# FFN up: three pairs of slabs in seven products before each ordinary pair, where seven-product and ordinary pairs alternated

## The reference

```python
h = x @ w_up                                   # 512 x 1024 by 1024 x 5632
h = conv(h, conv_w, width 3, causal, per channel) + conv_b
gate, val = split(h, 2)
out = (silu(gate) * val) @ w_down              # 2816 x 1024
```

## Time and profile before

| what | us |
|---|---|
| median of three executions | 2039.16 |
| the profiled execution | 2042.29 |
| its span | 2040.6 |
| TensorE busy | 2026.4 |
| VectorE busy | 1619.3 |
| ScalarE busy | 1115.0 |
| GpSimd busy | 433.7 |

### The profile page before, as it was taken

How to read it: one execution, slowest core, us unless ns; L and a number is a source line. 1 busy time by engine, 2 the same in 40 slices (tenths; PEclk the granted TensorE clock), 3 DMA queues, 4 the chain that set the end, 5 groups by cost and what they waited for, 6 DMA issues and landing times.

```text
span 2040.6 us, 33333 instructions
## 1 busy us (share of the span) xinstructions
PE 2026.4 (99%) x12636; PEld 1750.7 (86%) x12636; DVE 1619.3 (79%) x2555; ACT 1115.0 (55%) x1861; POOL 433.7 (21%) x482
## 2 busy tenths in 40 slices
PE   9999999999999999999999999999999999999998
PEld 8889998888988899888877888998888889999887
DVE  6668878889467887899888669777997668877898
ACT  4755545447335555546656646555465755545555
POOL 0520332210000232120035402322110520332220
PEclk9999999999999999999999999999999999999999
DMA  8123344384432334467421123334674122334393
GB/s 291 64 104 125 109 130 150 121 255 172 145 129 75 97 105 129 145 190 243 166 73 42 63 83 104 119 104 155 197 237 163 65 104 83 109 122 147 115 269 122
DMA packets 82570, 276.42 MB, mean 135 GB/s; under 512 B 9408, under 2 KB 13632, under 8 KB 82032
## 3 DMA queue, kind: packets, MB, share of 16 engines
q1 hardware_dynamic: 59184, 214.67, 30.4%
q0 software_dynamic: 11200, 24.12, 5.8%
q10 hardware_dynamic: 12032, 35.54, 4.8%
HBM read 256.43 MB, written 14.73 MB: 133 GB/s over the span
## 4 chain that ended last, share of the span: by engine, by line
PE 91%; DVE 5%; DMA 2%; ACT 1%; issue 0%; DVEq 0%; ACTq 0%; SPq 0%
PE ps L2437 12%; PE ps L2438 12%; PE ps L2439 12%; PE ps L2649 6%; PE ps L3018 5%; PE ps L3019 5%; PE ps L3020 5%; PE ps L2976 5%; PE ps L2978 5%; PE ps L2977 5%; PE ps L2509 2%; PE ps L2465 2%; PE ps L2466 2%; PE ps L2467 2%; DMA raw<-slabs 2%; PE ps L2497 1%
## 5 line engine op out<-in xcount | busy, mean ns | idle before, releaser
L2437 PE MATMUL ps<-h_hi,w_hi 128*128 128x512 f32 (+1 forms) x1104 | 433.0, 392 | 0.0
L2438 PE MATMUL ps<-h_lo,w_hi 128*128 128x512 f32 (+1 forms) x1104 | 429.6, 389 | 0.0
L2439 PE MATMUL ps<-h_hi,w_lo 128*128 128x512 f32 (+1 forms) x1104 | 428.9, 389 | 0.0
L1603 DVE TENSOR_TENSOR w_lo<-raw,w_hi 128x1024 fp32r<-128x1024 f32 x300 | 372.0, 1247 | 39.1 <-ACT w_hi L901 35.5
L901 ACT ACTIVATE w_hi<-raw 128x1024 fp32r<-128x1024 f32 x312 | 326.4, 1053 | 133.1 <-DVE raw L2251 74.0
L2437 PEld LDWEIGHTS ps<-h_hi,w_hi 128*128 128x128 f32 x1104 | 207.6, 188 | 44.0 <-issue 4.0
L2439 PEld LDWEIGHTS ps<-h_hi,w_lo 128*128 128x128 f32 x1104 | 207.3, 188 | 43.2
L2438 PEld LDWEIGHTS ps<-h_lo,w_hi 128*128 128x128 f32 x1104 | 207.7, 188 | 38.9
L1281 ACT ACTIVATE work<-ps,conv_sb 128x512 f32<-128x512 f32 x120 | 93.0, 775 | 162.6 <-PE ps L2439 133.2
L3018 PE MATMUL ps<-w_hi,h_hi 128*128 128x512 f32 x408 | 159.7, 391 | 2.1 <-DVE w_lo L1603 2.1
L3020 PE MATMUL ps<-w_hi,h_lo 128*128 128x512 f32 x408 | 158.8, 389 | 0.0
(11 more groups left out here) (365 smaller groups left out, 5054.6 us busy)
## 6 DMA issues: line engine op xcount, KB each, us to landing
raw<-slabs SPq DMA_DIRECT2D x368, 512.0 KB, 4.1
act<-slabs POOLq DMA_DIRECT2D x64, 256.0 KB, 5.6
bias<-slabs SPq DMA_DIRECT2D x16, 512.0 KB, 6.3
x_dram<-x ACTq DMA_DIRECT2D x16, 512.0 KB, 5.0
x<-x_dram ACTq DMA_DIRECT2D x16, 512.0 KB, 4.9
raw<-act POOLq DMA_DIRECT2D x28, 256.0 KB, 3.3
act<-slabs SPq DMA_DIRECT2D x12, 512.0 KB, 5.4
bias_dram<-bias_rows ACTq DMA_DIRECT2D x2, 2048.0 KB, 12.3
```

The source lines that it names most:

```text
L1603: ve.tensor_tensor(w_lo[:, c % RING, :], raw[:, raw_slot(c), :], w_hi[:, c % RING, :].bitcast(f32), ALU.subtract).then_inc(lo_made, 1)
L2437: pe.matmul(ps[:, bank, cols], hi, h_hi[:, k, cols], start=k == 0, stop=False)
L2438: pe.matmul(ps[:, bank, cols], hi, h_lo[:, k, cols], start=False, stop=False)
L2439: last = pe.matmul(ps[:, bank, cols], lo, h_hi[:, k, cols], start=False, stop=k == KT - 1)
```

## The change

Pairs 7, 11 and 15 of each layer become seven-product pairs too: 4, then the groups 6-7-8-(9), 10-11-12-(13), 14-15-16-(17), in which the pair in brackets is ordinary. TensorE's products of neighbouring seven-product pairs are interleaved (lists at the end of the diff), and four pairs of PSUM banks are used in turn. The orders of ScalarE and VectorE are written anew as `first_period` (pairs 4 and 5 and the start of the first group), `period` (twice) and `last_period` (the last group and the end of the stage to pair 21). SP's loads follow the new order. GpSimd starts the sums for FFN down only when the adding transfer issued before them has landed (`landed`). One wait for `up_mm` is added to `split_hi`, one for `up_x3` to `x2`, and the negated convolution weights are made in four instructions instead of one. Shown are the core of the diff and the starts of the long lists; `part_hi`, `part_lo`, `copy`, `c11`, `c22` and `c12` do what they did, with their counts adapted.

```diff
 FAST, FAST_END = 4, 18
-FASTS = (FAST_END - FAST) // 2
+FAST_RUNS = 6, 10, 14
+IN_GROUP = 3
+FAST_PAIRS = [FAST] + [q + e for q in FAST_RUNS for e in range(IN_GROUP)]
+FASTS = len(FAST_PAIRS)
+X1_ORDER = [FAST] + [q + e for q in FAST_RUNS for e in (1, 0, 2)]
+UP_PRODUCTS = [(FAST, p) for p in (1, 2, 6, 4, 3)] + [
+    (q + e, p) for q in FAST_RUNS for e, p in (
+        (0, 1), (0, 2), (0, 6), (1, 1), (1, 2), (0, 4), (0, 3), (1, 6), (2, 1), (1, 4), (2, 2), (1, 3), (2, 6),
+        (2, 4), (2, 3))]
 PARTS = "a11", "x1", "x2", "x3", "x4"
 STEPS = FFT // 2
...
 
-            return (0 if q // 2 % 2 else 4) + e
+            return 2 * ((q + 2) % 4 if FAST <= q < FAST_END else q % 2) + e
...
+                def load(q, e):
+
+                    c = up_slab(L, q, e)
+                    if q - 2 not in FAST_PAIRS:
+                        sp.wait_ge(lo_made, made(c - RAW))
+                    elif e:
+                        sp.wait_ge(part_lo_made["x3"], part_count(L, q - 2, "x3"))
+                        sp.wait_ge(part_lo_made["x4"], part_count(L, q - 2, "x4"))
+                    else:
+                        sp.wait_ge(part_lo_made["x1"], part_count(L, q - 2, "x1"))
+                        sp.wait_ge(up_x2, fast(L, q - 2) + 1)
+                        sp.wait_ge(up_x3, fast(L, q - 2) + 1)
+                    sp.dma_start(raw[:, raw_slot(c), :], slabs[dram(c)]).then_inc(raw_in[raw_slot(c)], 16)
+
...
-            def down_sums(L, j):
+            def down_sums(L, j, landed=None):
...
                     pool.wait_ge(in_lo, 4 * (L + 1))
+                if landed:
+                    pool.wait_ge(up_x4, 16 * (fast(L, landed) + 1))
...
+                fourth_sum(L, 4)
+                down_sums(L, 0, 4)
+                fourth_sum(L, 6)
+                down_sums(L, 1, 6)
+                fourth_sum(L, 7)
+                fourth_sum(L, 8)
+                down_sums(L, 2, 8)
+                fourth_sum(L, 10)
+                down_sums(L, 3, 10)
+                fourth_sum(L, 11)
+                fourth_sum(L, 12)
+                down_sums(L, 4, 12)
+                fourth_sum(L, 14)
+                down_sums(L, 5, 14)
+                fourth_sum(L, 15)
+                fourth_sum(L, 16)
+                down_sums(L, 6, 16)
+                for j in range(7, STEPS - 1):
                     down_sums(L, j)
...
                     sc.wait_ge(w_used, 4 * i + (c - (RING + EARLY if early(c - RING) else RING) + 1))
+                if isinstance(i, int) and in_fast(c - RING):
+                    L, q, e = in_fast(c - RING)
+                    sc.wait_ge(up_mm, product_count(L, q, 2 if e else 3))
                 if isinstance(i, int) and summed(c):
...
+                def slab_tap(q, e):
+
+                    if q in FAST_PAIRS:
+                        sc.wait_ge(up_c, 3 * fast(L, q) + 2 + e)
+                        if not e:
+                            sc.wait_ge(up_mm, product_count(L, q, 4))
+                        sc.wait_ge(neg_made, 1)
+                    else:
+                        sc.wait_ge(w_used, up_slab(L, q, e) + 1)
                     if not e:
-                        sc.wait_ge(up_mm, 5 * fast(L, q) + 4)
                         sc.wait_ge(gated, FFT * L + q - 1)
-                    sc.wait_ge(neg_made, 1)
-                    scale = conv_sb[:, L, 2 * q + 1, 2:3] if e else conv_neg[:, L, (q - FAST) // 2, 2:3]
+                    turned = q in FAST_PAIRS and not e
+                    scale = conv_neg[:, L, fast(0, q), 2:3] if turned else conv_sb[:, L, 2 * q + e, 2:3]
                     sc.activation(work[:, q % 2, e * SEQ:(e + 1) * SEQ], ps[:, up_bank(q, e), :], ACT.Identity,
...
+                def first_period(f):
+
+                    split_hi(up_slab(L, f + 1))
+                    part_hi(f, "x3")
+                    slab_silu(f - 1)
+                    slab_tap(f - 1, 1)
+                    split_hi(up_slab(L, f + 1, 1))
+                    copy(f, 0)
+                    copy(f, 1)
+                    part_hi(f, "x4")
+                    copy(f, 2)
+                    part_hi(f + 2, "a11")
+                    part_hi(f + 3, "x1")
+                    part_hi(f + 2, "x2")
+                    slab_tap(f, 0)
+                    part_hi(f + 2, "x1")
+                    part_hi(f + 2, "x3")
+                    slab_silu(f)
...
+                def period(f):
+
+                    slab_tap(f, 0)
+                    slab_silu(f - 1)
+                    part_hi(f + 1, "x4")
+                    copy(f + 1, 2)
+                    part_hi(f + 2, "x1")
+                    part_hi(f + 2, "x2")
+                    copy(f + 2, 0)
+                    slab_tap(f, 1)
...
+                def slab_tap(q, e, tap):
+
+                    u = UP_SLABS * L + 2 * q + e + 1
+                    earlier, done, sh = ((tap1, tap0, 2), (tap2, tap1, 1))[tap]
+                    y = work[:, q % 2, e * SEQ + sh:(e + 1) * SEQ]
+                    turned = q in FAST_PAIRS and not e
+                    scale = conv_neg[:, L, fast(0, q), tap:tap + 1] if turned else conv_sb[:, L, 2 * q + e, tap:tap + 1]
+                    ve.wait_ge(earlier, u)
+                    ve.scalar_tensor_tensor(y, ps[:, up_bank(q, e), 0:SEQ - sh], scale, y, ALU.mult, ALU.add).then_inc(done, 1)
+
...
+                def first_period(f):
+
+                    split_lo(up_slab(L, f + 1))
+                    slab_tap(f - 1, 1, 1)
+                    slab_tap(f - 1, 1, 0)
+                    x1(f + 2)
+                    slab_gate(f - 1)
+                    split_lo(up_slab(L, f + 1, 1))
+                    x1(f + 3)
+                    c11(f)
+                    part_lo(f, "x4")
+                    c22(f)
+                    x2(f + 2)
+                    part_lo(f + 2, "a11")
+                    part_lo(f + 3, "x1")
+                    x3(f + 2)
...
+                def period(f):
+
+                    c12(f)
+                    slab_tap(f - 1, 1, 1)
+                    part_lo(f + 1, "x3")
+                    part_lo(f + 2, "a11")
+                    slab_tap(f - 1, 1, 0)
+                    c11(f + 1)
+                    part_lo(f + 1, "x4")
+                    c22(f + 1)
+                    x2(f + 2)
+                    slab_tap(f, 0, 1)
...
+                def last_period(f):
+
+                    slab_tap(f - 1, 1, 1)
+                    c12(f)
+                    part_lo(f + 1, "x3")
+                    part_lo(f + 2, "a11")
+                    slab_tap(f - 1, 1, 0)
+                    c11(f + 1)
+                    part_lo(f + 1, "x4")
+                    x2(f + 2)
+                    c22(f + 1)
+                    slab_tap(f, 0, 1)
...
...
+                def bank_free(q):
+                    if q >= FAST + 2:
+                        pe.wait_ge(tap0, UP_SLABS * L + 2 * q - 6)
+
+                def p1(q):
+                    bank_free(q)
+                    pe.wait_ge(part_lo_made["a11"], part_count(L, q, "a11"))
                     product(q, 0, 0, "a11", h_quarter(0, 0), True).then_inc(up_mm, 1)
+
+                def p2(q):
                     product(q, 1, 0, "a12", h_quarter(1, 0), True).then_inc(up_mm, 1)
-                    pe.wait_ge(up_copy, 3 * f + 1)
-                    pe.wait_ge(part_lo_made["x2"], f + 1)
+
+                def p6_p5(q):
+                    pe.wait_ge(up_copy, 3 * fast(L, q) + 1)
+                    pe.wait_ge(part_lo_made["x2"], part_count(L, q, "x2"))
                     pe.wait_ge(in_lo, 4 * L + 4)
                     product(q, 0, 0, "x2", in_parts(2), False, True).then_inc(up_mm, 1)
-                    pe.wait_ge(part_lo_made["x1"], f + 1)
+                    pe.wait_ge(part_lo_made["x1"], part_count(L, q, "x1"))
                     product(q, 1, 1, "x1", in_parts(0), True).then_inc(w_used, 1)
-                    pe.wait_ge(up_copy, 3 * f + 2)
-                    pe.wait_ge(part_lo_made["x3"], f + 1)
+
+                def p7(q):
+                    pe.wait_ge(up_copy, 3 * fast(L, q) + 2)
+                    pe.wait_ge(part_lo_made["x3"], part_count(L, q, "x3"))
                     product(q, 0, 0, "x3", in_parts(1), False, True).then_inc(w_used, 1)
-                    pe.wait_ge(tap0, UP_SLABS * L + 2 * q)
-                    forward(even + 2, 0, 2)
-                    pe.wait_ge(up_c, 3 * f + 2)
+
+                def p4(q):
+                    pe.wait_ge(up_c, 3 * fast(L, q) + 2)
                     product(q, 0, 0, "a22", in_parts(3), False, True).then_inc(up_mm, 1)
-                    pe.wait_ge(part_lo_made["x4"], f + 1)
+
+                def p3(q):
+                    pe.wait_ge(part_lo_made["x4"], part_count(L, q, "x4"))
                     product(q, 1, 1, "x4", h_quarter(1, 1), False, True).then_inc(up_mm, 1)
-                    forward(even + 3, 0, 3)
+
+                p1(FAST)
+                p2(FAST)
+                p6_p5(FAST)
+                p7(FAST)
+                bank_free(FAST + 1)
```

(121 more changed lines are left out.)

422 lines of the change are left out of this document (273 added, 149 removed).

## The result

The changed kernel takes 2055.24 us, the median of 4 runs (2054.09 to 2060.55); the kernel before took 2039.2 beside it (4 runs, 2037.84 to 2039.9). The ratio is 1.0085, 95% interval 1.0066 to 1.0103: slower by 16 us, where +2.3 was forecast, and above the range's upper end of 2050. The profiled execution is the slowest of the four, 2060.55 us, so its stages add up to some 5 us more than the median shows. The time lies above that of every rival too; the slowest of them was put at 2051.5.

The account below looks back on a forecast made before the run. TensorE, busy 2026.4 of 2040.6 us, was taken to set the time. The profiled 2042.29 - 10.6 + 12.1 + 0.8 = 2044.6, that is +2.3 us; against the median of 2039.16, 2041.5 us, range 2033 to 2050.

Parts of the forecast that it names:

- Term 1: FFN up, pairs 7, 11 and 15 of each layer: fewer products on TensorE, -10.6 us.
- the change isn't felt as such: Rival: the pairs that change kind wait for their own operands, so the 10.6 us gain is lost; 2051 us, chance 0.05.
- Term 2: First period of each layer: ScalarE's copy for pair 4 comes late, so TensorE's p6 waits 3.03 us; +12.1 us.
- copy isn't late: Rival: p6 doesn't wait for ScalarE's copy; 2029.4 us, or 2035.5 with half the stall; chance 0.15 for both.
- Term 3: Seams between groups in FFN up: operands slightly late, 0.1 us for each of eight seams, +0.8 us.
- The seams break: Rival: GpSimd's sums and a later landing hold VectorE, c22 and p4 0.9 us late in 12 groups; 2051.5 us, chance 0.20.
- The stage end: End of FFN up, pairs 17 to 21: VectorE's load is light and splits lead their forwards, so no wait; nothing.
- The landing wait: GpSimd's five sums held until the adding transfer lands, 3.3 us after issue; put at nothing.

Follow-up runs that it names:

- e9: e5 with GpSimd's five sums for FFN down cut from 256 to 8 columns each, so the network isn't computed: 2036.08 us.
- e2: The kernel before with only the new ScalarE order in pair 4's period, both splits, silu and tap ahead of the first copy: 2057.81 us.
- e1b: e1 with c22 of pair 6 put ahead of a tap and the part x2 of pair 7 in VectorE's first_period: 2052.07 us.
- e1: The changed kernel with both copies of pair 4 back ahead of the second split, the first also ahead of the silu, in ScalarE's first_period: 2050.43 us.
- e5: e1b with ScalarE's first copy of pair 6 also put ahead of the silu of pair 4: 2042.38 us.
- e10: e5 with VectorE's x1 of pair 8 behind c22 of pair 6, and c22 earlier at the seams and in the last group: 2039.75 us.
- e11: e10 with ScalarE's last tap and split put back ahead of operand 3 and the silu in last_period: 2035.28 us.
- e12: The kernel before with operand 3 put ahead of the last tap in ScalarE's order, the silu left in place: 2044.12 us.
- e3: The changed kernel without the wait of GpSimd's sums for the landing of the adding transfer: 2059.82 us.
- e6: e5 with VectorE's c11 and c22 of pair f+4 ahead of x3 of pair f+5 and a tap at the seam: 2044.19 us.
- e7: e6 without the wait of GpSimd's sums for the landing: 2054.78 us.

## Why the prediction was wrong

**Term 1, -10.6: right.** e9 shows 10.1 of it, and the pitch of 0.12 us stayed at full clock. The rival *the change isn't felt as such* (Term 1 lost) falls.

**Term 2, +12.1: the wait right, its price wrong.** The copy started at 211.67, 5.5 us after p1 as forecast; the waits sum to 12.3 by starts. The term took TensorE's standing still for the whole price, and put what the clock does at nothing without a reason. At each of the four waits the granted clock went to half, for 3.4 us in three layers and 6.8 in layer 2: 6.7 us more, 19.0 for the term in place of 12.1. e2 measures the same edit alone, with the clock's fall in three layers of four: 18.2 us. The rival *copy isn't late* falls.

The walk also ended at the first stall. The same order, a copy behind a silu that waits for VectorE's taps, came again two pairs later (e1b). The second stall cost nothing while the first stood, so this omission isn't in the 16 us; it would have misled whoever took out the first stall only, as e1 did.

**Term 3, +0.8: too small.** It is 3.4 us in the changed kernel; without the stalls e5 minus e9 is 6.3 us for what the sums do in all groups together. The mechanism was named (GpSimd beside VectorE, 0.53 us an operation), and was put at nothing in the sum: I took the case of the earlier trace rows, a split that isn't lengthened, as the rule. In that case it was the other engine that waited: the sum beside the split took 1.64 us, and GpSimd's sums of this size take 0.74 where nothing holds them. At the seam shown VectorE has 1.9 us more to do, against 1.0 in hand. *The seams break* had this mechanism and even its 1.6 us, but its price is wrong as well: where c22 was late, TensorE waited 0.4 us at most and not 0.9, in three places of the changed kernel and seven of e5 and not in twelve groups. A stretch of 41 us in layer 0, one group's length, of the changed kernel (each engine's busy us and instructions, granted clock, DMA):

```profile
267.00:308.00 41.00, 41.00 (x300) 38.98 (x299) 38.99 (x56) 23.45 (x39) 13.02 (x13) 1.00 0.41 123
```

VectorE is busy for 39.0 us of it, over the 37.9 of my count; in e9 (266 to 307) it is 36.8.

**The stage end, "I expect no wait": wrong.** I counted VectorE's load there and the lead of each split over its forward in FFN up, and stopped at the stage's edge. The step moved ScalarE's operand and silu past the last tap, and what that delays is a split of FFN down. It costs 4.5 us in e10 (against e11), and the operand alone 2.9 in the kernel before (e12). No wait came before a forward of pairs 17 to 21 but small ones: the changed kernel's trace has 0.31 us for a `w_lo` before pair 17's in layer 0.

**The landing wait, at nothing: right in that it costs nothing.** Taking it away gains nothing in the changed kernel (e3), and costs 10.6 us where the stalls are gone (e6 to e7): it keeps GpSimd's sums off VectorE's x3 of pair 6.

The sum again, from the two profiled executions: -10.1 + 12.3 + 6.7 + 3.4 = 12.3 us in FFN up, 4.8 behind it and 0.8 ahead of the first p1, which is the 17.9 by which the spans differ (2058.5 - 2040.6); the medians differ by 16.0. Of the 4.8, 2.4 are waits for FFN down's `w_lo`; the rest isn't taken apart. Term 3 is smaller here than the 6.3 of e5 and e9, since the waits for c22 at pair 6 come only once both stalls are gone.

What stays open: why the clock fell at ten of the twelve waits of 2.9 us in the changed kernel, e2 and e3 and not at the other two, at five of the thirteen waits of 1.7 to 2.4 us at pairs 6 and 7 in e1, e1b, e3 and e7, and for twice as long in layer 2 of three kernels. e10 has no wait for c22 left, one of 0.6 us for a split, and still 2.1 us of "up" over e9. An order that keeps the sums off all splits wasn't tried.

## What to carry to other kernels

Where an engine is busy for 99% of the span, a new stall of a few microseconds costs its length and, often, what the clock takes behind it, here half as much again; look at the granted clock beside every gap. In lists that engines work through in a fixed order, moving one instruction is to be followed past the stage's edge, and taking out one stall is to be followed to the next: the first late copy gave back 5 us alone, both together 13. And where a duration beside another engine looks unchanged, read that engine's durations too before calling the overlap free: one of the two had waited. Such an operation is to be costed at the longest duration the trace has for it, wherever less is in hand than the difference.

## What was not expected of the hardware

After 2.9 us of standing still in layer 0 TensorE took up its work at full clock, and the granted clock fell only 0.5 us later, for 3.4 us; a wait of 2.12 us was followed by the same in e1b, and two of 1.8 us in layers 1 and 2 there by none. GpSimd's sums of 256 columns lengthened VectorE's splits from 1.22 to 1.76 and from 0.68 to 1.22 us where both began with one landing, and in e7 one sum of VectorE took 3.43 us in place of 0.69 beside four of GpSimd's operations in a row.
